# Two-layer hybrid transformer with mixture of experts: when the rows and the residual for the closing normalisation are loaded

## The reference, cut to what matters

```
hl = _layer_norm(xl) * (1.0 + sc2) + sh2
ml = _expert_choice_ffn(hl, w_router[l], w_exp_gate[l], w_exp_up[l], w_exp_down[l])
xl = _layer_norm(alpha * xl + g2 * ml, ln2_g[l], ln2_b[l])
if need_ctx:
    hc = _layer_norm(xc) * (1.0 + csc2) + csh2
    mc = _expert_choice_ffn(hc, w_router[l], w_exp_gate[l], w_exp_up[l], w_exp_down[l])
    xc = _layer_norm(alpha * xc + cg2 * mc, ln2_g[l], ln2_b[l])
```

## Time and profile before

| | |
|---|---|
| median of 3 runs | 3648.82 us |
| lowest and highest run | 3645.45 and 3655.16 us |
| profiled execution, first to last instruction | 3654.0 us |
| mean granted TensorE clock | 0.957 of full speed |
| TensorE matmul busy | 3354.7 us (92%) |
| VectorE busy | 2261.8 us (62%) |
| ScalarE busy | 1699.2 us (47%) |
| GpSimd busy | 692.9 us (19%) |
| DMA moved | 632.90 MB |

### The profile page before, as it was taken

The page is one execution under the profiler, slowest core; times in us unless marked ns, Lnnn a source line. Parts: engine busy times, 40 slices in busy tenths (PEclk is TensorE's granted clock), DMA queues, the critical chain, the costliest instruction groups (busy, mean ns, idle before and its releaser), DMA issues.

```text
span 3654.0 us, 50651 instructions
## 1 busy us (share of the span) xinstructions
PE 3354.7 (92%) x19492; PEld 2846.1 (78%) x19492; DVE 2261.8 (62%) x3338; ACT 1699.2 (47%) x2165; POOL 692.9 (19%) x494
## 2 busy tenths in 40 slices
PE   7998899899999979999998499998999969999995
PEld 4997569799999857777776388677888857878784
DVE  3686750621221649999997584842413358999997
ACT  3113752522121247777775522743322127777774
POOL 3001012223322012222222200112244201111111
PEclk9999999999999979999999699998999979999998
DMA  7242024012221339999998222131133218999995
GB/s 255 98 145 99 25 93 150 24 47 99 92 82 66 113 120 336 331 331 333 335 335 300 76 81 81 47 99 47 36 110 103 93 70 296 356 349 355 354 356 207
DMA packets 331991, 632.90 MB, mean 173 GB/s; under 512 B 14558, under 2 KB 104974, under 8 KB 325422
## 3 DMA queue, kind: packets, MB, share of 16 engines
q1 hardware_dynamic: 309056, 557.88, 44.2%
q0 software_dynamic: 22768, 72.68, 6.0%
HBM read 614.00 MB, written 16.50 MB: 173 GB/s over the span
## 4 chain that ended last, share of the span: by engine, by line
PE 66%; DVE 15%; ACT 6%; issue 6%; DMA 5%; POOL 0%; ACTq 0%; DVEq 0%; SPq 0%; POOLq 0%
PE ps L878 42%; PE ps L1303 13%; DVE part L2231 4%; DMA raw<-in_w_exp_gate 2%; PE ps L1009 2%; PE ps L1041 2%; DVE hx L2231 2%; DVE area L2239 1%; PE ps L1027 1%; DVE area L1826 1%; ACT hx L1620 1%; ACT area L1365 1%; ACT area L1459 1%; PE ps L1029 1%; DMA raw<-in_w_exp_down 1%
## 5 line engine op out<-in xcount | busy, mean ns | idle before, releaser
L878 PE MATMUL ps<-hx,part 128*128 128x384 f32 (+2 forms) x4704 | 902.5, 352 | 10.3 <-POOL part L539 5.5
L878 PEld LDWEIGHTS ps<-hx,part 128*128 128x128 f32 x4704 | 831.5, 189 | 77.0 <-issue 7.6
L1303 PE MATMUL ps<-part,hx 128*128 128x512 f32 x3072 | 750.6, 397 | 19.9 <-ACT part L1620 8.9
L1303 PEld LDWEIGHTS ps<-part,hx 128*128 128x128 f32 x3072 | 574.6, 190 | 154.2 <-issue 13.4
L2231 DVE TENSOR_TENSOR part<-raw,part 128x2048 fp32r<-128x2048 f32 x256 | 598.3, 2338 | 29.4 <-ACT part L1620 28.3
L1620 ACT ACTIVATE part<-raw 128x2048 fp32r<-128x2048 f32 x256 | 490.2, 1916 | 149.0 <-DMA raw<-in_w_exp_up 73.7
L539 POOL TENSOR_TENSOR part<-raw,part 128x2048 fp32r<-128x2048 f32 x68 | 314.4, 4623 | 752.8 <-ACT part L536 750.9
L1303 PE MATMUL ps<-hx 128*128 128x512 f32 x1536 | 384.8, 400 | 13.1 <-ACT hx L1620 9.6
L1303 PEld LDWEIGHTS ps<-hx 128*128 128x128 f32 x1536 | 289.6, 190 | 90.0 <-ACT hx L1620 13.0
L878 PE MATMUL ps<-part,hx 128*128 128x256 f32 (+2 forms) x2208 | 317.0, 306 | 12.8 <-DVE part L2213 6.0
L2231 DVE TENSOR_TENSOR hx<-raw,hx 128x2048 fp32r<-128x2048 f32 x128 | 294.7, 2302 | 49.3 <-ACT hx L1620 47.6
(11 more groups left out here) (280 smaller groups left out, 3681.0 us busy)
## 6 DMA issues: line engine op xcount, KB each, us to landing
raw<-in_w_exp_gate SPq DMA_DIRECT2D x128, 1024.0 KB, 6.0
raw<-in_w_exp_up SPq DMA_DIRECT2D x128, 1024.0 KB, 6.4
raw<-in_w_exp_down SPq DMA_DIRECT2D x128, 1024.0 KB, 6.6
raw<-in_w_mod SPq DMA_DIRECT2D x48, 1024.0 KB, 6.6
raw<-in_w_in SPq DMA_DIRECT2D x44, 1024.0 KB, 5.4
raw<-in_w_gate SPq DMA_DIRECT2D x32, 1024.0 KB, 5.5
area<-in_bias POOLq DMA_DIRECT2D x32, 512.0 KB, 4.2
raw<-in_w_branch SPq DMA_DIRECT2D x16, 1024.0 KB, 5.2
```

What stands on the lines that cost most here:

```text
L878: last = mm(dst, a, b, start=i == 0, stop=i == len(pairs) - 1)
L1303: last = mm(ps[:, bank, :], x, y, start=kh == 0 and a == 0, stop=kh == 1 and a == len(pairs) - 1)
```

## The change

The POOL engine waits, before the loads of `rows2` and `x2v`, until the last weight block of the last expert has landed in its ring slot. In layer 1 the load of the context's gate row is left out, and VectorE's wait in the closing of layer 1 counts three loads instead of four. No value that is computed changes.

```
                 pool.wait_ge(*S("xg", l).at(2 * E))
+                last = B_EXP[l] + EXP_BLOCKS * E - 1
+                pool.wait_ge(ring_in[last % RING], 16 * (last // RING + 1))
                 for v, src in enumerate((mod_d[l, 0:1, 5 * D:6 * D], mod_d[l, 1:2, 5 * D:6 * D],
                                          A["ln2_g"][l:l + 1, :], A["ln2_b"][l:l + 1, :])):
-                    load(rows2[:, v, :], src.to_broadcast([P, D])).then_inc(*S("rows2_in", l).by(16))
+                    if v != 1 or full == NT:
+                        load(rows2[:, v, :], src.to_broadcast([P, D])).then_inc(*S("rows2_in", l).by(16))
                 for t in range(full):
                     load(x2v[:, t, :], x1_d[t]).then_inc(*S("x1_in", l).by(16))
...
                 if l == DEPTH - 1:
-                    dve.wait_ge(*S("rows2_in", l).at(64))
+                    dve.wait_ge(*S("rows2_in", l).at(48))
```

## The result

The changed kernel takes 3629.02 us (median of 4 runs, 3625.09 to 3632.85) beside 3651.99 us for the kernel before (4 runs, 3645.45 to 3658.53). The ratio is 0.994, 95% interval 0.9928 to 0.9952: 17.5 to 26.3 us faster. The forecast was 3626.7 us and 22.1 us faster.

A forecast was written before the change was run, and what follows sets the result against it. DMA engines were taken as nearly always busy in both expert stages. Gains of 13.3 + 0 in layer 1 and 11.3 - 2.5 = 8.8 in layer 0 make 22.1: 3648.8 - 22.1 = 3626.7 us, range 3619 to 3640.

The forecast's parts named there:

- The stream set free: Last expert of each layer: loads leave its weight stream, gaining 13.3 us in layer 1 and 11.3 in layer 0.
- Layer 1, the loads in time: Layer 1 closing: seven loads from 3598.8 take 14.3 us, land at 3613.1 with 2.1 us to spare, so wait 0.
- Layer 0, the wait: Layer 0 closing: ten loads beside projection blocks take 23.7 us from 1971.5, land at 1995.2; closing waits 2.5 us.
- I take 2.5: Layer 0: closing ready at 1992.7 waits 2.5 us for loads; 0 if the projection blocks were no hindrance.
- The barrier costs nothing.: End of expert stage: POOL, its loads issued by 1977 and 3602.6, is at the barrier long before the others.
- the case of operations that meet the splits earlier: Layer 0 closing, 2.5 us late, meets POOL's splits one or two operations earlier: nothing, bounds 2 us more or 1 less.
- The context row: Layer 1: leaving out 0.52 MB gives nothing on the path, 1.3 us if the cover of about 2 us were gone.
- The signs: Profile after: POOL's first loads near 1971.5 and 3590, gate wait at most 2 us, full clock, closings near 1995 and 3606.
- One sign of being wrong: Either layer: the closing starts on a DMA more than 3 us after the barrier.
- rival 1: Closing waits replace the stall: up to 6 us more in layer 0, 3.5 in layer 1, plus 2; 3638; chance 0.12.
- Rival 2: Last expert gains in one layer only or none, something else holding it: gain 0 to 11, 3638 to 3649; chance 0.09.
- Rival 3: VectorE holds back POOL's transfers until idle: closings 7.5 and 1.0 us later, 8.5 slower, 3657; chance 0.04.

The follow-up runs named there:

- two one-layer runs: Kernel before with the wait on the last weight block added in one layer alone, all rows loaded: ratio 0.9974 with layer 1, 0.9971 with layer 0.
- no_drain: Changed kernel, but GpSimd signals the barrier at the end of the expert stage with a small memset instead of its drain: ratio 0.9945 to the kernel before.
- l1_only: Kernel before with the wait on the last weight block added in layer 1 alone, all four rows loaded in both layers: ratio 0.9974.

## Why the prediction was right, and where it was not

**The stream set free.** Right in both layers: expert 15 loses nothing once the loads are gone, and the two one-layer runs show that it was the loads. Read off expert 13 of the same trace the gain was 13.3 and 11.3, and this pair of profiles gives 13.34 and 11.26. As the price of the old placement the 13.3 was a little large: it was taken from one execution, in which the clock fell a second time in layer 1. Between the means of the profiles, three with the wait and three without, layer 1 gains 11.3.

**Layer 1, the loads in time.** Right. Seven loads were to take 14.3 us alone and land 2.1 us before the closing. The last was issued at 3585.3 and no residual load of layer 1 took over 9.9 us (L838 in 3570 to 3600, below), so they were down by 3595.2, 13.1 us from the first issue, which leaves 2.4.

```profile
DMA to landing us min/median/max: 7.7/8.8/9.9
```

**Layer 0, the wait.** The 23.7 us for ten loads beside the projection blocks were nearly right: from the first issue at 1970.38 to the last landing at 1993.2 is 22.8, and the drain that waits for it ends at 23.5. The term that was mis-sized is the wait of the closing, "I take 2.5": it is 4.3 (40.89 less the 36.6 at which the closing could start). What came later is the first issue, 17.1 us after the first down block where 15.3 was taken. Of these 1.8 us, 0.5 are b11's later issue, 0.8 its own way, 7.3 us instead of 6.5, and 0.5 the step from its landing to GpSimd's first issue, which the prediction put at nothing. Together with the layer 1 term this overstates the gain by about 3 us against the means of the profiles, 19.0. That the median came within 2.4 us of 3626.7 is therefore partly luck.

**"The barrier costs nothing."** This step was wrong in its mechanism and cheap in its price. POOL issued its last load early but was not at the barrier; its drain stood 19.26 us until the loads had landed, and held ScalarE too. no_drain shows it. It costs nothing that can be measured here, because VectorE needs the same loads anyway. It did move POOL's splits along with the closing, so that the very same two operations were slow as before, and the case of operations that meet the splits earlier did not arise.

**The context row.** Nothing in time, as forecast; l1_only shows that without it the cover in layer 1 is just gone.

**The signs.** b11 at 20.5 us, the gate wait under 2 us (0.5), the full clock and the first loads of layer 0 near 1971.5 (1970.38) came as written. The positions in layer 1, near 3590 and 3606, were 3582.14 and 3597.65; the 8 us between are the scatter outside the stretches. The closing of layer 0 at 1994.16 was to be released by a DMA and was released by the drain. One sign of being wrong was a closing on a DMA more than 3 us after the barrier. Read by its letter it did not come, since the barrier itself was late; by its sense it did, the closing of layer 0 waited 4.3 us for its loads, and in no_drain 5.26 us for the DMA itself.

**The rivals.** The wait in layer 0 came out 1.8 us longer, of the up to 6 that rival 1 allowed. Rival 2 is refuted by the two one-layer runs. Rival 3, VectorE holding back POOL's transfers: the seven loads of layer 1 went out while VectorE was at its last splits and were down in 13.1 us, where the earlier trace rows have 12.8 for six and a small one with VectorE almost idle. So VectorE did not hold them back visibly. The rule of the Trainium skill, "SBUF — State Buffer", section "SBUF: two separate sides", speaks of two-port operations such as a copy in float32 within SBUF. The prediction applied it to this kernel's splits and additions, which have two inputs each, and nothing here shows that the rule means them. So the prediction's remark that the trace does not agree says too much; no stretch read here has a copy of the kind that it names beside such a transfer.

## What to carry to other kernels

A transfer that is not wanted yet still costs its bytes while the DMA engines are full, and more than its bytes when the stall lets TensorE's clock fall; look for what is issued inside the full stretch and wanted after it. The price can be read before anything is built if a twin of the disturbed piece, here the odd expert before, lies in the same trace, but take more than one execution of it. Once the transfers are out of the way, what they share the engines with decides when they land: put them ahead of what is not urgent, in one queue, rather than starting them earlier in another. Here that took the wait out of the stretch; in the time of the whole kernel it is not shown.

## What the runs showed of the hardware that was not expected

GpSimd's drain waits until the transfers that GpSimd issued have landed: 19.26 us of drain behind ten loads, ended 0.6 us after the last landing, and without it the barrier falls 0.2 us after the last addition. Transfers of two queues share the full DMA engines so that a start 6.1 us earlier left the closing at 40.7 us from the first down block instead of 40.9. And the same stall of layer 1 cost 3.2 us more in one execution than in the other for the same bytes: half of it is a longer wait for one block (5.47 or 3.82 us), half a second fall of the granted clock (24 matmuls in 7.33 or in 5.74 us). In layer 0 it was the other execution whose clock fell a second time. Last, a row broadcast to 128 partitions took longer than a plain load of the same 512 KB: in layer 1 of the changed kernel the three rows landed 3.8, 5.3 and 6.7 us after issues about 0.55 us apart, that is about 2.0 us one behind the other, and the four residual loads behind them about 1.3 us.
